# Scattering the last expert outputs by column halves, and taking two tiles' norm moments on ScalarE, in a hybrid attention and MoE encoder step

## What is computed

```python
def moe_layer(x, ...):
    scores = sigmoid(x2 @ router_w)            # 64 experts, 8 groups, top 8 of the best 4 groups
    ...
    routed = sum over chosen experts e of  wts_e * ((silu(x @ w_gate[e]) * (x @ w_up[e])) @ w_down[e])
    shared = (silu(x2 @ sh_gate) * (x2 @ sh_up)) @ sh_down
    return routed + shared

# layer 0: hybrid mixer -> layer_norm 0 -> MoE -> layer_norm 1
# layer 1: pooling mixer (pool_w * pool_scale) -> layer_norm 2 -> MoE -> layer_norm 3
x = layer_norm(ALPHA * x + sublayer(x), g, b)  # mean and variance over the 1024 columns
```

## Time and profile before

| | |
|---|---|
| median of 3 runs | 1411.6 us (1409.34 to 1413.28) |
| profiled execution | 1412.18 us, of which the profile's span is 1410.4 us |
| TensorE busy | 1334.8 us, 95% of the span |
| VectorE busy | 613.8 us, 44% |
| ScalarE busy | 333.9 us, 24% |
| GpSimd busy | 52.3 us, 4% |
| expert stretch of layer 0 / layer 1 | 254 to 779.8 us / 868 to 1393.8 us |

### The profile page before, as it was taken

One profiled execution on the slowest core, in us unless ns is written; L12 is line 12 of the kernel. 1 busy time (PEld: TensorE's weight loads), 2 busy tenths in 40 slices (PEclk: granted clock), 3 DMA queues, 4 the chain that ended last, 5 costly groups with the idle time before them and its releaser, 6 DMA issues.

```text
span 1410.4 us, 17804 instructions
## 1 busy us (share of the span) xinstructions
PE 1334.8 (95%) x6542; PEld 692.4 (49%) x6542; DVE 613.8 (44%) x1197; ACT 333.9 (24%) x674; POOL 52.3 (4%) x95
## 2 busy tenths in 40 slices
PE   6988989999999999999999689999999999999994
PEld 4556546544444544444443565444455444445432
DVE  0766266343334343333343774333434333343436
ACT  1633321222212222222212132222222222222111
POOL 6101010000000000000000300000000000000000
PEclk9999989999999999999999979999999999999998
DMA  9412128699989989998999424999899989989981
GB/s 277 119 56 74 32 92 319 236 388 388 389 358 394 388 345 422 396 387 341 410 398 376 172 90 172 367 386 384 349 408 388 392 360 410 374 355 407 396 329 34
DMA packets 72113, 435.68 MB, mean 309 GB/s; under 512 B 12915, under 2 KB 15075, under 8 KB 22016
## 3 DMA queue, kind: packets, MB, share of 16 engines
q1 hardware_dynamic: 69248, 428.13, 76.6%
q0 software_dynamic: 2816, 6.87, 1.6%
HBM read 433.23 MB, written 1.76 MB: 308 GB/s over the span
## 4 chain that ended last, share of the span: by engine, by line
PE 92%; DVE 5%; ACT 2%; issue 1%; DMA 1%; SPq 0%; DVEq 0%
PE bank L875 32%; PE bank L798 18%; PE bank L830 16%; PE bank L824 13%; PE bank L782 3%; PE bank L1207 3%; PE bank L995 1%; PE bank L885 1%; PE bank L958 1%; DVE sb_x L1659 1%; PE bank L1286 1%; DVE sb_ln_st L1651 1%; DVE sb_x L1655 1%; DMA sb_x<-in_x_sample_dram 1%; DVE sb_yl L1594 1%
## 5 line engine op out<-in xcount | busy, mean ns | idle before, releaser
L1588 DVE TENSOR_TENSOR sb_x<-sb_x,bank 128x512 f32<-128x512 f32 (+1 forms) x396 | 242.0, 679 | 108.8 <-PE bank L824 108.8
L830 PE MATMUL bank<-sb_wslot,sb_ht 128*64 128x512 f32 x1024 | 231.0, 593 | 0.0
L875 PE MATMUL bank<-sb_wslot,sb_xg_own 128*64 128x512 f32 x1024 | 226.5, 595 | 1.8 <-ACT sb_xg_own L1338 1.8
L875 PE MATMUL bank<-sb_wslot,sb_xt 128*64 128x512 f32 x1024 | 226.8, 595 | 0.0
L1607 DVE TENSOR_TENSOR sb_hh<-sb_sg,bank 128x256 f32<-128x256 f32 x64 | 27.0, 421 | 375.8 <-ACT sb_sg L1360 375.8
L824 PE MATMUL bank<-sb_yh,sb_place 128*128 128x512 f32 x396 | 158.6, 400 | 10.1 <-DVE sb_yl L1594 10.1
L1594 DVE SCALAR_TENSOR_TENSOR sb_yl<-bank,sb_gslot,sb_yh 128x512 fp32r<-128x512 f32 x128 | 96.1, 751 | 162.7 <-ACT sb_yh L1344 162.7
L824 PE MATMUL bank<-sb_yl,sb_place 128*128 128x512 f32 x396 | 156.4, 395 | 0.0
L1360 ACT ACTIVATE sb_sg<-bank 128x256 f32<-128x256 f32 x64 | 24.6, 384 | 556.7 <-PE bank L875 556.7
L830 PEld LDWEIGHTS bank<-sb_wslot,sb_ht 128*64 128x64 f32 x1024 | 72.8, 137 | 144.6 <-issue 139.3
L798 PE MATMUL bank<-sb_pick,sb_xh 128*128 128x512 f32 x384 | 142.9, 401 | 0.0
(11 more groups left out here) (303 smaller groups left out, 1043.6 us busy)
## 6 DMA issues: line engine op xcount, KB each, us to landing
sb_wslot<-in_moe_w_gate_dram SPq DMA_DIRECT2D x64, 2048.0 KB, 8.5
sb_wslot<-in_moe_w_up_dram SPq DMA_DIRECT2D x64, 2048.0 KB, 13.3
sb_wslot<-in_moe_w_down_dram SPq DMA_DIRECT2D x64, 2048.0 KB, 15.7
sb_w_in_hi<-in_w_in_dram SPq DMA_DIRECT2D x2, 2048.0 KB, 14.5
sb_w_in_lo<-in_w_out_dram SPq DMA_DIRECT2D x1, 4096.0 KB, 12.8
sb_w_in_lo<-in_w_in_dram SPq DMA_DIRECT2D x2, 1024.0 KB, 11.1
sb_ln_g<-in_ln_g_dram POOLq DMA_DIRECT2D x4, 512.0 KB, 4.8
sb_ln_b<-in_ln_b_dram POOLq DMA_DIRECT2D x4, 512.0 KB, 6.1
```

What stands on the lines that cost most here:

```text
L830: last = pe.matmul(y_b[c][64 * e:64 * e + 64, :], ht[:, k, 64 * e:64 * e + 64], w_down[u][:, e, k * D + c * 512:k * D + (c + 1) * 512], st ...
L875: last = pe.matmul(gu_b[64 * e:64 * e + 64, :], xgt[b][:, k, sl], w_gu[u][:, :, e, k * FE:(k + 1) * FE], start=k == 0, stop=k == DK_SLICES ...
L1588: dve.tensor_tensor(dst, dst, banks.tile[order[f]][0:rows, :], ALU.add).then_inc(s["added"], 1)
```

## The change

Four parts. (1) In pairs 4 to 7 of the last body, `place_add` and `add_sums` go through the six sums by column half (tiles 0, 1, 2 of half 0, then of half 1) instead of by tile, so the first three sums wait only for half 0 of `yl`; they use banks 7, 2, 3, 6, 7, 2, and no down product behind them waits for an add. (2) The same order, with banks 7, 2, 3, 4, 5, 0, in the scatter behind the last pair. VectorE's fourth body is written out for this. (3) In norms 1 and 3, mean and sum of squares of tiles 1 and 2 come from two ScalarE instructions each (`moments`), with their accumulated output; VectorE leaves out `bn_stats` and `bn_aggr` there and waits for the root ahead of its first instruction on the tile. (4) GpSimd clears the strip of `xt` after norm 1's tile 2, no longer before it, since ScalarE uses `xt` as scratch.

```diff
+HALF_SUM_BANKS = (7, 2, 3, 6, 7, 2)
+END_SUM_BANKS = (7, 2, 3, 4, 5, 0)
...
+def sums_of(m, last):
+
+    if last and m >= QUAD:
+        return HALF_SUM_BANKS, True
+    return (LAST_SUM_BANKS if m == BODY - 1 else SUM_BANKS), False
+
+
+def fill(f, by_half):
+
+    return (f % TILES, f // TILES) if by_half else divmod(f, 2)
...
+def by_act(n, t):
+
+    return n % 2 == 1 and t > 0
...
-                    gp.wait_ge(var_ready, 4)
+                    gp.wait_ge(x_ready, 6)
                     gp.memset(xt[:, :, T_COLS:], 0.0).then_inc(s["init"], 1)
-
-                    gp.wait_ge(x_ready, 6)
...
-                pe.wait_ge(s["y_ready"], 2 * i + 1)
+            def place_add(u, i, order, by_half):
+
+                pe.wait_ge(s["y_ready"], 2 * i + (0 if by_half else 1))
                 pe.wait_ge(s["place_copied"], i + 1)
                 for f in range(FILLS):
-                    t, c = divmod(f, 2)
+                    t, c = fill(f, by_half)
+                    if by_half and f == TILES:
+                        pe.wait_ge(s["y_ready"], 2 * i + 1)
...
                     if m == BODY - 1:
-                        pe.wait_ge(s["added"], FILLS * i + 2)
-                        down_pair(u, i, n, FILLS * i + 6)
+                        if by_half:
+                            down_pair(u, i, n)
+                        else:
+                            pe.wait_ge(s["added"], FILLS * i + 2)
+                            down_pair(u, i, n, FILLS * i + 6)
...
-            place_add(1, total, (7, 4, 5, 2, 3, 0))
+            place_add(1, total, END_SUM_BANKS, True)
...
+                def moments(t):
+                    rows = ROWS[t]
+                    mean, var = ln_mv[0:rows, t, 0:1], ln_mv[0:rows, t, 1:2]
+                    act.wait_ge(s["added"], FILLS * PAIRS * rounds + TILES + t + 2)
+                    step(act.activation(xt_all[0:rows, 0:D], x[0:rows, t, :], ACT.Copy, scale=-1.0 / D, accum_out=mean))
+                    step(act.activation(xt_all[0:rows, 0:D], x[0:rows, t, :], ACT.Square, bias=mean, accum_out=var))
...
+                moments(1)
+                ln_sqrt(2 * l + 1, 0)
+                root(1)
+                moments(2)
+                root(2)
...
+                    if by_act(n, t):
+                        dve.wait_ge(sd_ready, 3 * n + t + 1)
+                        step(dve.scalar_tensor_tensor(out=xr, in0=xr, scalar=ln_mv[0:rows, t, 0:1], in1=ln_g[0:rows, :],
+                                                      op0=ALU.add, op1=ALU.mult))
+                        step(dve.reciprocal(ln_rs[0:rows, t:t + 1], ln_sd[0:rows, t:t + 1]))
+                        step(dve.scalar_tensor_tensor(out=xr, in0=xr, scalar=ln_rs[0:rows, t:t + 1], in1=ln_b[0:rows, :],
+                                                      op0=ALU.mult, op1=ALU.add), x_ready)
+                        continue
```

More of the change, by code:

```diff
@@ L293, in second, with variances @@
     return slice(64 * half, 64 * half + 64) if t == 2 else slice(0, P)
+def by_act(n, t):
+    return n % 2 == 1 and t > 0
+def variances(n, t):
+    return sum(1 for m in range(n + 1) for u in range(TILES if m < n else t + 1) if not by_act(m, u))
 def xt_part(i):
@@ L1381, in act_experts @@
                 turns(r, GROUPS // 2 - 1, (0,))
+            return rounds
         @block.scalar
@@ new lines, in turns @@
+            def turns(r, j, last):
+                for m in range(BODY):
+                    b, q, u = m // QUAD, m % QUAD, m % 2
+                    i = 2 * (r * TURNS + 4 * j + m // 2) + u
+                    if q == 0:
+                        dve.wait_ge(s["place_done"], i + 1)
+                        pick_group(1 - b, bass.ds(16 * j + 8 * b + 8, GROUP_E) if not last else slice(16 * j + 8 * b + 8, 16 * j + 8 * b + 8 + GROUP_E))
+                    dve.wait_ge(s["sg_ready"], i + 1)
+                    dve.tensor_tensor(hh[:, :], sg[:, :], gu_b[:, FE:2 * FE], ALU.mult).then_inc(s["h_ready"], 1)
+                    if m:
+                        low_out(1 - u, i - 1)
+                    dve.wait_ge(s["place_copied"], i + 2)
+                    for e in range(2):
+                        h, c0 = slice(64 * e, 64 * e + 64), P + 2 * (2 * q + e)
+                        dve.tensor_reduce(gslot[h, u, :],
+                                          place_b[h, 0:TILES * PLACED].rearrange("p (t n) -> p t n", t=TILES)[:, :, c0:c0 + 2],
+                                          AX.XY, ALU.add).then_inc(s["gate_ready"], 1)
+                    add_sums(i, *sums_of(m, last))
+                    if m == BODY - 1:
+                        low_out(u, i)
@@ L1620, in dve_experts @@
+            with dve.Fori(0, rounds) as r:
+                with dve.Fori(0, GROUPS // 2 - 1) as j:
+                    turns(r, j, False)
+                turns(r, GROUPS // 2 - 1, True)
                 dve.tensor_scalar(pos_x[:, :, :], pos_x[:, :, :], -float(SLOTS), None, ALU.add).then_inc(s["next_round"], 1)
                 dve.wait_ge(s["next_round"], r + 1)
-            add_sums(PAIRS * rounds, (7, 4, 5, 2, 3, 0))
+            add_sums(PAIRS * rounds, END_SUM_BANKS, True)
             dve.wait_ge(s["added"], FILLS * (PAIRS * rounds + 1) + 1)
```

39 lines of the change are left out of this document (11 added, 28 removed).

## The result

The changed kernel took 1403.62 us in the median of four runs (1401.45 to 1404.33), beside 1412.44 us of the kernel before on the same chip: a ratio of 0.9929, with a 95% interval of 0.9918 to 0.9941, or 10.0 us less (8.3 to 11.6). The profiled execution took 1401.45 us with a span of 1399.6, against 1412.18 and 1410.4. A second measurement gave 1403.07 us (six runs), ratio 0.9924 (0.9907 to 0.9941). So the change makes the kernel faster, but 13.3 us were forecast and some 10 came: the median lies 5.3 us above the forecast of 1398.3.

What follows compares the result with a forecast made beforehand. TensorE, with 92% of the chain, was taken to bound the kernel. 5.9 us between the layers plus 7.4 us behind layer 1 (4.0 + 3.4) made 13.3 us, giving 1398.3 us from a median of 1411.6; range 1396.0 to 1402.2.

Steps and rivals of the forecast that it cites:

- Parts 1 and 2: Pairs 4 to 7 and the scatter behind the last pair: 4.0 us less in each layer (3.5 to 4.2).
- `m` = 7: Last pair of the bare group: the next product starts at 1382.90 instead of 1384.07, 1.15 us gained.
- the last scatter: Behind the last pair: VectorE's adds start earlier, 0.5 us taken, between nothing and 0.7 us.
- three rivals: Weights late (1405.3 us, chance 0.04), slower from late VectorE code (0.02), no effect in the bare group (1404.2 us, 0.05).
- Part 3 behind layer 1: Norm 3: VectorE loses 1.71 us on each of tiles 1 and 2, so the last store moves 3.4 us.
- Part 3 and 4 between the layers: Norm 1: TensorE's second pooling products start at 785.0 instead of 790.9, 5.9 us gained.
- the landing: Norm 1: `pool_scale` lands at 781.0 instead of 782.05, after tile 0 is done at 780.35; bounds 779.7 and 782.05.
- shared read path: Rival in norm 1: `pool_scale` lands before tile 0 is done, GpSimd goes first; 11.1 us in all, 1400.5; chance 0.19.
- the clock: Second pooling products in norm 1: a lower granted clock would cost up to 3.2 us; nothing was taken.

Runs made afterwards that it cites:

- scale_at_tile0: The changed kernel with GpSimd's scaling of the pooling weights held back by a wait until tile 0 of norm 1 is done; 1401.12 us, ratio 0.9913.
- pool_first_before: The kernel before with one edit, the pooling loads issued one down load earlier; 1411.2 us, ratio 0.9977.
- pool_first_halves: The changed kernel with the pooling loads one down load earlier and without ScalarE's moments in both norms; 1403.96 us, ratio 0.9927.
- pool_first: The changed kernel with the three pooling loads issued ahead of layer 1's first down load; 1399.01 us, ratio 0.9901; repeated: 1399.83 us, ratio 0.9898.
- moments_alone: The changed kernel with the scatter by tiles as before, keeping the moments of tiles 1 and 2 on ScalarE; 1410.35 us, ratio 0.9974.
- after_again: The changed kernel unaltered, measured and profiled a second time; 1403.07 us, ratio 0.9924.
- halves_alone: The changed kernel with all moments back on VectorE, keeping the scatter by halves; 1407.44 us, ratio 0.996.
- norm3_only: The changed kernel with ScalarE's moments in norm 3 alone, VectorE having its bn_stats back in norm 1; 1403.86 us, ratio 0.9932.
- halves_again: The changed kernel with all moments back on VectorE, the same kernel as halves_alone, run for a second profile; 1406.7 us, ratio 0.9951.

## Why the prediction was wrong

**Parts 1 and 2** were right in mechanism and a little large. The step from pair to pair shrank by 0.745 us, not 0.8; `m` = 7 gave 1.14 of 1.15; the last scatter gave 0.41 of 0.5, as the adds wait 0.31 us for VectorE's own subtraction. Together 3.79 and 3.75 us in the two layers, 4.0 forecast in each. TensorE waits a short while for adds, none of VectorE's straight code is late, and no load is: three rivals are out.

**Part 3 behind layer 1** was right: 3.4 us forecast, and the last store is issued 10.59 us behind the last add, before 13.96 (1397.06 - 1386.47 and 1407.77 - 1393.81). The last store moved by 10.71 us: these 3.4, the 3.75 of layer 1's bare group and last scatter, and 3.59 by which layer 1's experts start earlier (864.64 against 868.23). ScalarE's moments took 1.06 and 1.15 us and the reads 0.19, where 1.1 and 0.19 were taken.

**The step that failed is "Part 3 and 4 between the layers", 5.9 us.** In the first profile it gave 3.66. It fell in two places; in that profile the first alone makes the whole difference, as its second block is at full clock.

First, the landing. The prediction said of the load of `pool_scale` that "the DMA engines are saturated ... so I expect that it can't move by the whole", and took 781.0. The load was issued 2.34 us sooner (764.16 against 766.50) and landed 3.09 us sooner, at 778.96. The reading was of one window behind the issue, 780 to 785. Windows of the kernel before ahead of it show that the DMA engines had run short of work there, so what is issued later can move with the experts (why it moved by 0.75 us more than its issue, no run shows):

```profile
745.00:750.00 5.00, 5.00 (x25) 1.53 (x22) 1.17 (x2) 1.07 (x2) 0.00 (x0) 1.00 0.81 336
750.00:755.00 5.00, 4.15 (x19) 2.92 (x21) 3.67 (x8) 1.34 (x3) 0.00 (x0) 1.00 0.79 272
```

In every profile with this order of loads and no added wait the scaling begins 2.3 to 3.7 us behind the last add, and tile 0 is done at 4.5 at the earliest; the forecast needed a beginning later than 4.5. This is the rival "shared read path", which the prediction gave 0.19: it had put the second block at 787.15 and the whole gain at 11.1 us, where the profile has 787.25 and 10.7. With GpSimd in front, the table's third column says what happened: in the kernels with `bn_stats` VectorE is held 2.0 to 2.1 us, in those with ScalarE's moments 3.7 to 4.0. The statistics of tile 1, 1.71 us, had been work that VectorE could do while GpSimd had the read path. Left out, they only leave a longer hold, and tile 1 is done 11.1 to 11.3 us behind the last add with them or without. That is the rule of the Trainium skill (SBUF — State Buffer, section "Who interferes with whom") that the prediction had named as speaking against the change; the first eight lines of the table agree. So between the layers the moments gave nothing at tile 1, and the 3.7 us there are those of the bare group and the scatter alone.

Second, the clock, for which the prediction took nothing ("TensorE will by then have worked 4 us, about as long as before"). scale_at_tile0 puts the landing's error right and has tile 1 at the forecast's 9.2 us, yet its second block takes 5.86 us, and 2.0 of the 2.2 us won are lost again. Its granted clock is 0.50, the lower of the two levels (1.2 GHz), until 788. The same block is at full clock in some profiles that start it at 11.2 to 11.4 us and partly at the lower one in others.

pool_first_before and pool_first_halves have next to no hold (0 and 0.2 us) and no slow block: their second block starts at 9.1 and 9.3 us, takes 3.84, and the scaled products start 14.0 and 14.1 us behind the last add, which is where the forecast's sum had them. In pool_first and its repetition VectorE is done sooner still, at 7.8 and 8.3, but the 48 records take 7.88 and 8.34 us at a mean clock of 0.70 and 0.65, and the scaled products start at 14.0 and 15.0. So for the stretch up to there nothing third is missing. That pool_first lies 14.0 and 14.4 us below the kernel before by its two ratios, near the 13.3 forecast for the change alone, is in part luck: its first profile has 1.4 us from the router's stretch.

The rows order the second block's clock by the idle time ahead of it: 3.84 us in the five profiles with 0.9 to 1.25 us of it, 5.47 to 6.48 in the six with 2.5 to 4.5 us. Where tile 0 is held, the first block comes late and the gap is short (before, changed, moments_alone); where it escapes, the gap is long (after_again, both of halves_alone, norm3_only). So one kernel comes out at 16.2 or 17.6 us, by which of two close events comes first: in the first profile `pool_scale` landed 0.16 us ahead of L1717, in after_again 0.39 us behind its start. These 1.4 us are most of the 1.8 us between the two profiles' spans. The first profile is that of the fastest of its four runs, 2.2 us below their median, so a slow second block may be part of what the other three lost; they have no profile, and it stays open. scale_at_tile0 alone breaks the order (0.76 us idle, 5.86 us long), though pool_first_before starts both blocks at the same distances with 0.90 us between them and is fast. That stays open.

By medians the moments in norm 1 are worth next to nothing: the changed kernel is 3.8 and 3.6 us faster than halves_alone and halves_again, of which norm 3 is 3.4; norm3_only is 0.2 to 0.8 us slower than the changed kernel, less than its interval. So by time alone a gain of up to 1.7 us there is not shut out; that there is none at tile 1 rests on the table.
